# A gated linear recurrence on Trainium2: the products of block totals move from DVE to POOL

## The reference

```
G = cumsum(log_f)                                   # (L, 128)
decay[i, j] = exp(G[i] - G[j]) for j <= i, else 0   # per key channel
A[i, j] = sum_k q[i, k] * k[j, k] * decay[i, j, k]
o = A @ v + (q * exp(G)) @ S
S_new = exp(G_last) * S + (k * exp(G_last - G)).T @ v
```

## Time and profile before

| what | us |
|---|---|
| median of 3 runs | 3292.36 (3288.82 to 3296.77) |
| the profiled execution | 3299.27 |
| its span in the trace | 3297.5 |
| PE busy | 3061.6 |
| DVE busy | 1717.1 |
| ACT busy | 923.7 |
| POOL busy | 305.8 |

### The profile page before, as it was taken

One profiled execution on the slowest core, in us unless ns is written; L12 is line 12 of the kernel. 1 busy time (PEld: TensorE's weight loads), 2 busy tenths in 40 slices (PEclk: granted clock), 3 DMA queues, 4 the chain that ended last, 5 costly groups with the idle time before them and its releaser, 6 DMA issues.

```text
span 3297.5 us, 42945 instructions
## 1 busy us (share of the span) xinstructions
PE 3061.6 (93%) x17124; PEld 2693.1 (82%) x17124; DVE 1717.1 (52%) x2311; ACT 923.7 (28%) x1490; POOL 305.8 (9%) x473
## 2 busy tenths in 40 slices
PE   6999999988898797775899999998999999899999
PEld 4888779857888696775799898978999998688887
DVE  4422542127897685885344454444444445355554
ACT  3222312214554462112222222223222222232221
POOL 1200220001000003663000000000000000000000
PEclk9999999988998897997999999999999999999999
DMA  4322332222100322333122121232121212322221
GB/s 166 121 107 105 128 111 87 97 64 56 27 25 10 91 59 82 109 110 136 58 84 77 52 77 52 77 116 102 52 77 52 77 52 93 107 97 77 83 97 40
DMA packets 205462, 271.24 MB, mean 82 GB/s; under 512 B 46984, under 2 KB 146764, under 8 KB 205264
## 3 DMA queue, kind: packets, MB, share of 16 engines
q1 hardware_dynamic: 205264, 268.50, 24.2%
HBM read 211.43 MB, written 57.03 MB: 81 GB/s over the span
## 4 chain that ended last, share of the span: by engine, by line
PE 50%; DMA 1%; DVE 1%; ACT 1%; issue 0%; SPq 0%; POOL 0%; POOLq 0%; ACTq 0%
PE mf_psO L1625 27%; PE mf_psT L1663 22%; DMA mf_nat<-scratch_mix 1%; PE mf_psT L1611 1%; DVE mf_wlo L1512 0%; ACT mf_whi L1442 0%; DVE mf_hs L1541 0%; DVE mf_acc L1535 0%; ACT mf_xhi L1457 0%; ACT mf_hs L1466 0%; DVE mf_xlo L1525 0%; DVE mf_acc L1582 0%; SPq L1387 0%; POOL mf_rstd L1433 0%; SPq L1418 0%
## 5 line engine op out<-in xcount | busy, mean ns | idle before, releaser
L1582 DVE TENSOR_TENSOR mf_acc<-mf_psO,mf_acc 128x1024 f32<-128x1024 f32 x272 | 332.9, 1224 | 384.9 <-PE mf_psO L1625 384.9
L1663 PE MATMUL mf_psT<-mf_xhi,mf_whi 128*128 128x384 f32 (+1 forms) x1536 | 492.8, 321 | 15.3 <-issue 9.9
L1663 PE MATMUL mf_psT<-mf_xhi,mf_wlo 128*128 128x384 f32 (+1 forms) x1536 | 492.2, 320 | 0.0
L1663 PE MATMUL mf_psT<-mf_xlo,mf_whi 128*128 128x384 f32 (+1 forms) x1536 | 492.2, 320 | 0.0
L1625 PE MATMUL mf_psO<-mf_whi,mf_uhi 128*128 128x512 f32 (+1 forms) x1088 | 426.6, 392 | 0.0
L1625 PE MATMUL mf_psO<-mf_whi,mf_ulo 128*128 128x512 f32 (+1 forms) x1088 | 425.8, 391 | 0.0
L1625 PE MATMUL mf_psO<-mf_wlo,mf_uhi 128*128 128x512 f32 (+1 forms) x1088 | 425.6, 391 | 0.0
L1442 ACT ACTIVATE mf_whi<-mf_st 128x2048 fp32r<-128x2048 f32 x108 | 201.8, 1909 | 640.0 <-PE mf_psO L1625 613.8
L1663 PEld LDWEIGHTS mf_psT<-mf_xhi,mf_whi 128*128 128x128 f32 x1536 | 290.5, 189 | 18.7 <-issue 15.9
L1663 PEld LDWEIGHTS mf_psT<-mf_xlo,mf_whi 128*128 128x128 f32 x1536 | 290.5, 189 | 1.8
L1663 PEld LDWEIGHTS mf_psT<-mf_xhi,mf_wlo 128*128 128x128 f32 x1536 | 290.3, 189 | 0.0
(11 more groups left out here) (179 smaller groups left out, 4868.3 us busy)
## 6 DMA issues: line engine op xcount, KB each, us to landing
mf_st<-in_w_up SPq DMA_DIRECT2D x48, 1024.0 KB, 5.6
mf_st<-in_w_down SPq DMA_DIRECT2D x48, 1024.0 KB, 4.8
pj_wst<-in_w_in SPq DMA_DIRECT2D x28, 1024.0 KB, 6.9
scratch_proj<-pj_ob SPq DMA_DIRECT2D x80, 256.0 KB, 2.0
mf_st<-in_w_o SPq DMA_DIRECT2D x12, 1024.0 KB, 6.1
pj_xin<-in_x_prompt SPq DMA_DIRECT2D x16, 512.0 KB, 3.9
mf_nat<-scratch_mix SPq DMA_DIRECT2D x16, 512.0 KB, 5.7
mf_xin<-in_x_prompt SPq DMA_DIRECT2D x16, 512.0 KB, 3.7
```

The costliest lines, as they stand in the source:

```text
L1582: nc.vector.tensor_tensor(acc[0:r, i, :], psO[k % 2][0:r, :], acc[0:r, i, :], ALU.add).then_inc(s["o_out"], 1)
L1663: last = nc.tensor.matmul(ps, wa[b4][:, w0:w0 + P], xa[:, j, c0:c0 + cn], start=j == 0 and q == 0, stop=j == KD - 1 and q == 2)
```

## The change

DVE's product of totals (line 1151) goes to POOL, where it stands right behind POOL's product on k of the same merge; it reads and writes the same elements. The waits that guard the reuse of the `tot` buffer of tile n - 3 at level 1 go with it: POOL now waits for the state of tile n - 3 (`s_out`) and for that tile's last product on q (`qp_ready`), ahead of its product on k. DVE still waits for the totals of the level below, which now come from POOL.

```diff
                     if i >= 2:
                         pool.wait_ge(s["tot_ready"], merge_no[n, i - 1] + 1)
+                    elif n >= NQ:
+
+                        pool.wait_ge(s["s_out"], n - NQ + 1)
+                        pool.wait_ge(s["qp_ready"], merge_no[n - NQ, levels(n - NQ)] + 1)
+                    hv = halves(n, m)
                     kv = pairs(k[n % NL], n, m)
                     nb = H * tiles[n][1] // (2 * m)
                     nc.gpsimd.tensor_tensor(kv[:, :, 0:m], kv[:, :, 0:m],
-                                            halves(n, m)[:, :, 1:2].to_broadcast([P, nb, m]),
+                                            hv[:, :, 1:2].to_broadcast([P, nb, m]),
                                             ALU.mult).then_inc(s["ks_ready"], 1)
+                    nc.gpsimd.tensor_tensor(totals(n, 2 * m).rearrange("p (b t) -> p b t", t=1), hv[:, :, 0:1],
+                                            hv[:, :, 1:2], ALU.mult).then_inc(s["tot_ready"], 1)
...
                 if i == 1:
                     dve.wait_ge(s["qp_begun"], n + 1)
-                    if n >= NQ:
-
-                        dve.wait_ge(s["s_out"], n - NQ + 1)
-                        dve.wait_ge(s["ks_ready"], merge_no[n - NQ, levels(n - NQ)] + 1)
                 else:
                     dve.wait_ge(s["tot_ready"], merge_no[n, i - 1] + 1)
                 qv, hv = pairs(qp[n % NQ], n, m), halves(n, m)
                 nc.vector.tensor_tensor(qv[:, :, m:2 * m], qv[:, :, m:2 * m],
                                         hv[:, :, 0:1].to_broadcast([P, nb, m]), ALU.mult).then_inc(s["qp_ready"], 1)
-                nc.vector.tensor_tensor(totals(n, 2 * m).rearrange("p (b t) -> p b t", t=1), hv[:, :, 0:1],
-                                        hv[:, :, 1:2], ALU.mult).then_inc(s["tot_ready"], 1)
```

## The result

| | before | after |
|---|---|---|
| median, us | 3290.59 (3287.16 to 3296.77, 4 runs) | 3308.75 (3304.66 to 3312.90, 4 runs) |
| ratio | | 1.0053, 95% interval 1.0032 to 1.0075 |
| the profiled execution, us | 3299.27 | 3312.90 |
| its span | 3297.5 | 3311.1 |

The changed kernel is slower, by 18.2 us at the medians, and the interval lies clear of 1. The page of its profile answers to the earlier trace rows: DVE's busy time fell by 47 us and POOL's rose by 28.

What follows compares the result with a forecast made beforehand. The prediction took a loop of hand-overs to bound the recurrence, its critical path being POOL's. 13 tiles x 1.2 us = 15.6 us, added to the median of 3292.4, gave 3308; range 3294 to 3320.

Steps and rivals of the forecast that it cites:

- The path: Recurrence, POOL's order from the power's end to the end of level 3's k-product: 5.98 us, with POOL last, not DVE.
- t1: Product of totals at merge level 1, 256 elements, on POOL between the k-products of levels 1 and 6: 0.71 us.
- t6: Product of totals at merge level 6, on POOL between level 6's k-product and the gate: 0.20 us.
- +1.2 us a tile: Even stretch of the recurrence: POOL's laid-out order from level 1's k-product through level 3's, 7.19 us against 5.98.
- k1's gain of 0.16: POOL's k-product of level 1, no longer held back by DVE's totals, would take 0.71 us instead of 0.87.
- The turns: DVE's q-products of levels 6, 2, 7 and 3, coming between POOL's instructions, each hold POOL up 0.3 us.
- About 13 times: How often the loss of 1.2 us a tile counts in the recurrence: 15.6 us in all.
- Rival D, the clock: TensorE's granted clock falls while PE idles: 12 us more (3320) with a dip every fourth tile, 3355 in every; chance 0.13.
- A: DVE is what binds; POOL's totals find room in its pauses: gain about 5 us, 3287; chance 0.08.
- B: The turns don't happen and DVE's q-products slip into PE's shadow: +0.3 us a tile, 4 us, 3296; chance 0.15.
- C, dearer totals: On POOL, t1 at 0.87, t6 at 0.39, totals of levels 2 and 7 uncovered by 0.2: 23 us, 3315; chance 0.14.
- Signs: Expected after: period 15.3 us, POOL busy about 11.7 of it, DVE down some 50 us, t1 0.7, gate 1.26.

Runs made afterwards that it cites:

- t34_twice: Changed kernel with POOL forming the totals of levels 3 and 4 twice, first into a spare buffer: period 14.93 us, median 3308.7 us, one run.
- t1_twice: Changed kernel with POOL forming the totals of level 1 twice, first into a spare buffer: period 15.41 us, median 3315.3 us, one run.
- t1_dve: Changed kernel with level 1's totals formed by DVE again: period 14.12 us, median 3289.3 us, ratio to before 0.9986 to 1.0011.
- t6_dve: Changed kernel with level 6's totals alone formed by DVE again: period 14.77 us, median 3305.2 us, one run.
- q_small: Changed kernel with DVE's q-products of levels 2, 6 and 7 replaced by a one-column copy: period 14.30 us, median 3287.0 us, one run.
- late_after: Changed kernel with POOL's mean and power, DVE's scaling and POOL's gate one spot later each: median 3307.8 us, ratio to before 1.0028 to 1.0057.

## Why the prediction was right

It gave 3308 us, slower, and 3308.75 was measured; the mechanism was right, and the sum came out closer than its terms deserve.

* *The path is POOL's, from power to k3, and the waits view names the wrong engine.* Right: t34_twice shows that load beside the path is free, t1_twice and t1_dve that the place between k1 and k6 isn't.
* *t1 and t6 lie on it, t2 to t5 and t7 don't.* Right, by t1_dve, t6_dve and t34_twice; t2, t5 and t7 were not tried alone.
* *+1.2 us a tile.* Too high; measured 0.81. Start to start, forecast and measured: k1 0.71 and 0.80; t1 0.71 and 0.57; k6 with q6's turn 0.92 and 0.76; t6 with q2's turn 0.50 and 0.42; gate 1.26 and 1.23; k2 with q7's turn 0.92 and 0.89; to k3's start 1.27 and 1.34; k3 0.90 and 0.91. Sum 7.19 and 6.92. The largest errors are q6's turn, put at 0.30 and about 0.18 by q_small, and the price of t1, taken from k1's form. 6.92 - 5.98 is 0.94 and not 0.81; 0.03 of it is that the 5.98 began at the power's end and not at k1's start, and 0.10 comes next. k1's gain of 0.16 isn't there: it took 0.87 before and 0.84 after with no total of DVE's beside it, so it had hardly been waiting for t1. And the 5.98 us of before were read in the shorter of its two kinds of tile, whose period is 14.02, 0.10 under the mean of 14.12.
* *The turns, 0.3 each.* Right in kind, 0.63 in place of 0.9 for the three (q_small).
* *About 13 times.* Right within one: 14 periods grew by 0.81, 11.3 us together, and the first, between the powers of the first two tiles, was 1.0 us shorter, as the dip of the kernel before lay in it.
* *Rival D, the clock.* It came beside the forecast: two dips, 2.1 us and not the 12 of the mild case, and one more dip in the kernel before. A dip costs 1.05, less than the 3.4 allowed: the two products and the transpositions took 1.5 us longer together, and 0.42 of that came out of the pause ahead of the second product, 0.23 and not 0.65. Nothing behind them was slower.
* *Rivals A and B.* Out: the period grew where A had it fall, and the turns happen (q_small). C, dearer totals: out, they were cheaper.
* *Signs.* Period 14.93 and not 15.3; POOL 11.23 us a tile (11.7 forecast); DVE down by 47 (50); gate 1.27 (1.26), t1 0.61 (0.7). PE's wait for k2 went from 0.92 to 1.41 us and is still put down to DVE.

Periods and dips make 11.3 - 1.0 + 2.1 = 12.4 us in the profiled execution; 15.6 were forecast, and the interval of the ratio stands for 10.5 to 24.7. That the median agrees to 0.75 us is luck: the base had been 3292.4 and is 3290.6 with the fourth run, and the difference came out at 18.2 where periods and dips account for 12.4.

## What to carry to other kernels

Before moving work to an engine with idle time, find where in its order the idle time lies. POOL had 4.7 us a tile free and none of it between the power and k2; 0.6 us put there (t1) cost 0.8, and 0.5 us put into the pause cost nothing. The same look finds what can leave: with power and gate moved off the path, the gate into the pause, a tile takes 1.0 to 1.2 us less than before.

When a wait names one of two operands, check the end of the other; and when instructions leave the critical place, ask what they now stand ahead of.

## What the runs showed of the hardware that I had not expected

POOL's product of 256 strided elements takes 0.61 us, 128 take 0.40, 64 0.29, 32 0.24, 16 0.21, 4 0.19: nearly a fixed price below 64. TensorE's granted clock fell in single tiles in which PE was never idle for more than 1.4 us at a stretch; it stayed at 1.00 in others laid out alike, and in all even tiles of late_after, with pauses of 1.57 us.
